# A decoder layer on one core: two per-feature row scales spread by a store and a broadcast read instead of by float32 matmuls with diagonals

## The reference, cut to what matters

```python
mod = silu(c) @ w_ada + b_ada                      # 6 rows of 1024
sh1, sc1, g1, sh2, sc2, g2 = split(mod, 6)
h = rms_norm(x, g_pre_mix) * (1 + sc1) + sh1
o_sb, o_mb, o_ds = three attention variants on h @ w_in      # 6 + 5 + 5 heads
g_sb, g_mb, g_ds = split(sigmoid(gate_logits + b_gate), 3)
merged = g_sb * (o_sb @ w_proj_sb) + g_mb * (o_mb @ w_proj_moba) + g_ds * (o_ds @ w_proj_dsa)
x = x + g1 * rms_norm(merged @ w_o, g_post_mix)    # the first row scale: g1 * g_post_mix
h = rms_norm(x, g_pre_ffn) * (1 + sc2) + sh2
gate, up = split(h @ w_up, 2)
x = x + g2 * rms_norm((silu(gate) * up) @ w_down, g_post_ffn)   # the second: g2 * g_post_ffn
```

## Time and profile before

| | |
|---|---|
| median of three runs | 485.15 us (483.96 to 485.51) |
| the profiled execution | 484.05 us, span on the core 482.3 us |
| TensorE busy | 453.0 us, 94% |
| TensorE's weight load busy | 411.3 us, 85% |
| VectorE busy | 299.8 us, 62% |
| ScalarE busy | 242.5 us, 50% |
| GpSimd busy | 60.4 us, 13% |
| DMA | 98.81 MB, mean 205 GB/s |

### The profile page before, as it was taken

One profiled execution on the slowest core, in us unless ns is written; L12 is line 12 of the kernel. 1 busy time (PEld: TensorE's weight loads), 2 busy tenths in 40 slices (PEclk: granted clock), 3 DMA queues, 4 the chain that ended last, 5 costly groups with the idle time before them and its releaser, 6 DMA issues.

```text
span 482.3 us, 8224 instructions
## 1 busy us (share of the span) xinstructions
PE 453.0 (94%) x3253; PEld 411.3 (85%) x3253; DVE 299.8 (62%) x487; ACT 242.5 (50%) x426; POOL 60.4 (13%) x96
## 2 busy tenths in 40 slices
PE   0959999999989998999999999999999999999994
PEld 0639999999878998998888799999999999999993
DVE  2056778878599968873779547672662464266215
ACT  5055554656656655667456237663353254335232
POOL 2000003000023220003769000000000000000000
PEclk9979999999999999999999999999999999999998
DMA  8998886696676566652466900997545735620002
GB/s 299 424 350 263 299 295 215 207 345 233 241 262 205 172 235 230 217 177 71 139 224 244 370 35 0 341 364 256 198 152 174 258 117 183 225 87 0 1 1 87
DMA packets 56370, 98.81 MB, mean 205 GB/s; under 512 B 5036, under 2 KB 41492, under 8 KB 53268
## 3 DMA queue, kind: packets, MB, share of 16 engines
q1 hardware_dynamic: 54036, 81.62, 49.4%
q0 software_dynamic: 2304, 16.78, 10.0%
HBM read 97.35 MB, written 1.05 MB: 204 GB/s over the span
## 4 chain that ended last, share of the span: by engine, by line
PE 86%; DVE 4%; DMA 4%; issue 2%; ACT 2%; SPq 1%; POOL 1%; DVEq 0%; ACTq 0%; PEldq 0%
PE psum L1163 26%; PE psum L1164 24%; PE psum L1165 24%; DMA ada_end<-in_w_ada_dram 4%; PE psum L1437 3%; DVE wlo L864 1%; PE psum L1390 1%; PE psum L1322 1%; PE psum L1259 1%; PE psum L1215 1%; PE psum L1257 1%; PE psum L1293 1%; PE psum L1226 1%; PE psum L1304 1%; POOL buft L540 1%
## 5 line engine op out<-in xcount | busy, mean ns | idle before, releaser
L1163 PE MATMUL psum<-hhi,whi 128*128 128x256 f32 (+1 forms) x680 | 196.8, 289 | 3.5 <-DVE hlo L968 2.7
L1164 PE MATMUL psum<-hlo,whi 128*128 128x256 f32 (+1 forms) x680 | 193.4, 284 | 0.0
L1165 PE MATMUL psum<-hhi,wlo 128*128 128x256 f32 (+1 forms) x680 | 193.2, 284 | 0.0
L1163 PEld LDWEIGHTS psum<-hhi,whi 128*128 128x128 f32 (+1 forms) x680 | 130.5, 192 | 8.4 <-issue 4.2
L1164 PEld LDWEIGHTS psum<-hlo,whi 128*128 128x128 f32 (+1 forms) x680 | 130.7, 192 | 0.3
L1165 PEld LDWEIGHTS psum<-hhi,wlo 128*128 128x128 f32 (+1 forms) x680 | 130.6, 192 | 0.0
L864 DVE TENSOR_TENSOR wlo<-raw,whi 128x1024 fp32r<-128x1024 f32 (+4 forms) x92 | 92.6, 1037 | 22.0 <-ACT whi L608 21.6
L608 ACT ACTIVATE whi<-raw 128x1024 fp32r<-128x1024 f32 (+4 forms) x92 | 74.3, 843 | 18.7 <-DMA raw<-in_w_in_dram 16.6
L1114 DVE TENSOR_TENSOR dlo<-draw,dhi 128x2048 fp32r<-128x2048 f32 x11 | 25.1, 2292 | 57.1 <-ACT dhi L783 57.1
L1109 DVE TENSOR_TENSOR wlo<-raw,whi 128x1024 fp32r<-128x1024 f32 x40 | 47.0, 1218 | 2.8 <-ACT whi L776 2.8
L783 ACT ACTIVATE dhi<-draw 128x2048 fp32r<-128x2048 f32 x11 | 20.9, 1914 | 43.9 <-PE psum L1165 43.9
(11 more groups left out here) (160 smaller groups left out, 593.7 us busy)
## 6 DMA issues: line engine op xcount, KB each, us to landing
raw<-in_w_up_dram SPq DMA_DIRECT2D x22, 1024.0 KB, 7.7
xn<-in_w_ada_dram POOLq DMA_DIRECT2D x16, 1024.0 KB, 5.2
raw<-in_w_in_dram SPq DMA_DIRECT2D x7, 2048.0 KB, 9.2
draw<-in_w_down_dram SPq DMA_DIRECT2D x11, 1024.0 KB, 5.3
raw<-in_w_in_dram SPq DMA_DIRECT2D x4, 1280.0 KB, 7.1
raw<-in_w_in_dram SPq DMA_DIRECT2D x3, 1536.0 KB, 6.9
raw<-in_w_ada_dram SPq DMA_DIRECT2D x2, 2048.0 KB, 9.8
ada_end<-in_w_ada_dram SPq DMA_DIRECT2D x4, 1024.0 KB, 17.0
```

What stands on the lines that cost most here:

```text
L1163: pe.matmul(dst, a[0], b[0], start=first, stop=False)
L1164: pe.matmul(dst, a[0], b[1], start=False, stop=False)
L1165: return pe.matmul(dst, a[1], b[0], start=False, stop=last)
```

## The change

Both row scales are written to a small tensor in device memory and read back with a broadcast over all partitions. GpSimd issues these DMAs: the store of the first scale in the unit loop at u = 27, behind the work of that unit; the store of the second after the loop; then both reads, once all heads are out, each behind a wait for its store. A store takes eight values from each partition, and their places in device memory are 128 floats apart, so all 1024 values stand alone; a read brings 4 KB to each of 128 partitions. The four diagonals, the four float32 matmuls, the four copies to `gb` and the waits between them are gone. VectorE waits for the arrival of the read before it first uses a scale.

```diff
--- before.py
+++ after.py
@@ -203,8 +203,6 @@
 MERGE_PIECES += [[(f // 2 + 2, 0), (f // 2 + 2, 1)] if f % 2 else [(f // 2 + 1, 2), (f // 2 + 1, 3)] for f in range(1, KC - 1)]
 MERGE_PIECES += [[(KC // 2 + 1, q) for q in range(4)]]
 
-SPREADS = [(1, 0, 0), (1, 0, 1), (2, 1, 0), (2, 1, 1)]
-
 VEC_GATE, VEC_ADA, VEC_PRE_MIX, VEC_POST_MIX, VEC_PRE_FFN, VEC_POST_FFN, VEC_END = (
     0, 3 * KC, 9 * KC, 10 * KC, 11 * KC, 12 * KC, 13 * KC)
 
@@ -283,7 +281,6 @@
         olo = sb("olo", [P, FULL_OCH, S], F32R, scope=mix)
         acc = sb("acc", [P, ADA_COLS], scope=mix)
 
-        spread = [acc[:, BANK * i:BANK * (i + 1)] for i in range(len(SPREADS))]
         mrow = sb("mrow", [P, BANK], scope=mix)
         wix = sb("wix", [P, TT, H_IX], scope=mix)
         dist = sb("dist", [P, CAUSAL], scope=mix)
@@ -344,7 +341,8 @@
         ss_ready, var_ready, sqrt_ready, xn_ready = sem("ss_ready"), sem("var_ready"), sem("sqrt_ready"), sem("xn_ready")
         x_turned, h_act, h_dve, h_hi, h_lo = sem("x_turned"), sem("h_act"), sem("h_dve"), sem("h_hi"), sem("h_lo")
         wix_turned, wix_ready, dve_scaled = sem("wix_turned"), sem("wix_ready"), sem("dve_scaled")
-        col_ready, diag_ready, m_spread, gb_ready = sem("col_ready"), sem("diag_ready"), sem("m_spread"), sem("gb_ready")
+        col_ready = sem("col_ready")
+        gain_out, gain_in = [None, sem("gain_out1"), sem("gain_out2")], [None, sem("gain_in1"), sem("gain_in2")]
         vec_in, vec_turned, vec_ready = sem("vec_in"), sem("vec_turned"), sem("vec_ready")
         logits, relu_ready, score_added, score_masked = (sem("logits"), sem("relu_ready"), sem("score_added"),
                                                         sem("score_masked"))
@@ -396,6 +394,9 @@
                 return [(P, slice(0, 3), every), (P, slice(3, 5), every), (P, slice(5, FULL_OCH), every),
                         (P, slice(FULL_OCH, N_OCH), every)]
             return [(P, slice(q, q + 1), every) for q in range(4)]
+
+        gain_dram = nc.dram_tensor("gains", (3, D), F32).ap()
+        GAIN_COLUMNS = [None, slice(0, KC), slice(KC, 2 * KC)]
 
         def hold(b):
 
@@ -523,6 +524,17 @@
                     pool.wait_ge(acc_done, n)
                 pool.dma_start(ada_part, ada_dram[:, n % KC, ADA_COLS * (1 + n // KC):ADA_COLS * (2 + n // KC)]).then_inc(part_in, 16)
 
+            def store_gain(g):
+
+                pool.wait_ge(col_ready, g + 1)
+                pool.dma_start(gain_dram[g, :].rearrange("(k p) -> p k", p=P), col[g][:, GAIN_COLUMNS[g]],
+                               allow_slow_non_contiguous=True).then_inc(gain_out[g], 16)
+
+            def load_gain(g):
+
+                pool.wait_ge(gain_out[g], 16)
+                pool.dma_start(gb[g][:, :], gain_dram[g:g + 1, :].to_broadcast([P, D])).then_inc(gain_in[g], 16)
+
             load_part(0)
             for u in range(N_UNITS):
                 if u == max(LOGITS_AT):
@@ -552,19 +564,14 @@
                     n = ADA_AT[u]
                     if n + 1 < 2 * KC:
                         load_part(n + 1)
-
-            def spread_diag(i):
-
-                g, vector, half = SPREADS[i]
-                pool.wait_ge(summed, 3)
-                pool.wait_ge(col_ready, g + 1)
-                for c in range(4):
-                    k = KC * vector + 4 * half + c
-                    ins = pool.tensor_scalar(spread[i][:, P * c:P * (c + 1)], ident[:, :], col[g][:, k:k + 1], -1.0, ALU.mult, ALU.mult)
-                ins.then_inc(diag_ready, 1)
-
-            for i in range(3):
-                spread_diag(i)
+                if u == max(min(COLUMNS_AT) + 1, ADA_UNIT[KC] + 1):
+                    store_gain(1)
+
+            store_gain(2)
+
+            pool.wait_ge(o_lo, N_HEADS)
+            load_gain(1)
+            load_gain(2)
 
             def merge_lo(f):
 
@@ -579,9 +586,7 @@
                 pool.wait_ge(gated, 3 * (f + 1))
                 pool.wait_ge(pool_step, f + 1)
                 pool.tensor_tensor(h32[:, f, :], g[0], g[2], ALU.add).then_inc(merged, 1)
-                if f == 0:
-                    spread_diag(3)
-                else:
+                if f:
                     merge_lo(f - 1)
             merge_lo(KC - 1)
 
@@ -759,10 +764,6 @@
                 act.wait_ge(merged, f + 1)
                 act.wait_ge(units, N_UNITS)
                 act.activation(hhi[:, f, :], h32[:, f, :], ACT.Copy).then_inc(m_hi, 1)
-                if 1 <= f <= len(SPREADS):
-                    g, _, half = SPREADS[f - 1]
-                    act.wait_ge(m_spread, f)
-                    act.activation(gb[g][:, BANK * half:BANK * (half + 1)], bank[6 + half][:, :], ACT.Copy).then_inc(gb_ready, 1)
             load_roots()
 
             def cut_up_hi(i, slot, q, first=False):
@@ -1094,7 +1095,7 @@
                     ins.then_inc(dve_scaled, 1)
 
                 if t == 0:
-                    dve.wait_ge(gb_ready, 2 * (k + 1))
+                    dve.wait_ge(gain_in[k + 1], 16)
                 gain(0)
                 if k == 0 and t == 1:
                     modulate(0)
@@ -1204,15 +1205,6 @@
                 for n in range(4):
                     mm = pe.transpose(bank[B_ROWS[g]][:, P * n:P * (n + 1)], mrow[:, P * n:P * (n + 1)], ident[:, :])
                 mm.then_inc(m_turned, 1)
-
-            def spread_gain(i):
-
-                pe.wait_ge(diag_ready, i + 1)
-                if i == 0:
-                    pe.wait_ge(o_lo, N_HEADS)
-                elif i >= 2:
-                    pe.wait_ge(gb_ready, i - 1)
-                pe.matmul(bank[6 + SPREADS[i][2]][:, :], neg1[:, :], spread[i], start=True, stop=True).then_inc(m_spread, 1)
 
             def turn_x(k, t):
 
@@ -1389,9 +1381,6 @@
                             pe.matmul(dst, w[0][:, ch, :], ohi[:, ch, :], start=False, stop=False)
                             mm = pe.matmul(dst, w[1][0:HD, ch, :], ohi[0:HD, ch, :], start=False, stop=True)
                 mm.then_inc(units, 1)
-                if 1 <= f <= len(SPREADS):
-                    spread_gain(f - 1)
-
 
             def out_part(t, half, n, kk):
 
@@ -1400,7 +1389,6 @@
                              [block_view(x[b % 2], b)[:, kk, BANK * n:BANK * (n + 1)] for x in (whi, wlo)],
                              k == 0, k == KC - 1)
 
-            pe.wait_ge(gb_ready, 4)
             for t in range(TT):
                 if t == 1:
                     pe.wait_ge(gated, 3 * KC)
```

## The result

The changed kernel takes 489.62 us (median of four runs, 488.31 to 493.79) against 484.99 for the kernel before (four runs); the ratio is 1.0107, 95% interval 1.0077 to 1.0136. It is slower by about 5 us, where 2.7 us less was forecast. The profiled execution took 489.13 us, span 487.4; that of before 484.05 and 482.3. The two differ by 5.1 us, and all of it is there at the join of TensorE and VectorE after the merge stage: the wait that ended at 267.35 ends at 272.46 (start, us, what, from the chain in order of time).

A forecast was written before the change was run, and what follows sets the result against it. TensorE's chain was taken as the bound, with VectorE and the first w_o load close behind: 3.40 us of matmuls removed, 2.7 us kept, added DMAs zero. 485.15 - 2.7 = 482.45, rounded to 482.4 us; 8-in-10 range 480.4 to 485.0.

The forecast's parts named there:

- What bounds the kernel, and what goes: Merge stage: TensorE's chain loses four gain matmuls, but the first w_o load's landing limits the gain to 2.7 us.
- the full 3.4: Merge stage: four gain matmuls of 0.85 us each, the 3.40 us TensorE alone would bring at the join.
- First store: Ahead of head 6's mask on GpSimd: 5.65 us of cover, so an issue of 4.3 us fits and costs nothing.
- Second store, the wait for its landing: GpSimd at 226.20 us: wait for landing at most 2.1 us after the issue ends; cost zero.
- the issue's cost D: GpSimd's time to issue one scattered store: 0.6 to 4.3 us, taken as about 1 to 2 us.
- my own formula: When the second store and reads free GpSimd: 226.20 + D + 2.1 + 0.54, so 229.4 to 233.1 us.
- the 233.6: Latest start, in us, of GpSimd's sum of tile 0 that still allows the w_o load at 239.5.
- The broadcast data: Two reads, 1.05 MB, beside the projection weights: 2.8 us of transfer, no cost taken, up to 1.4 us as bad end.
- the four that I had named as wrong: Store issue above 5.65 us; longer mask wait near 144; GpSimd in DMA work at 233.6; ScalarE awaiting weights near 234.
- (D): Slower: single-float issue of 8.4 us delays head 6 by 2.75 and the w_o load by 2.2; 490.1 us, chance 0.12.
- (C): Broadcast reads push the third projection block by 1.4 us, leaving 1.3 us saved; 483.85 us, chance 0.17.
- (A): The forecast itself: 2.2 to 3.0 us saved, 482.2 to 483.0 us, chance 0.47.

The follow-up runs named there:

- e1: Changed kernel with the second gain's store and read both moved behind GpSimd's last merge work; 482.10 us.
- e2: Changed kernel with stores as 128 runs of 32 bytes instead of 1024 single floats, all DMAs in place; 483.83 us.
- e4: Kernel before the change plus only the second gain's scattered store at 226 us, no read; 488.54 us.
- e3: Changed kernel with only the second broadcast read moved behind GpSimd's merge work, both stores kept; 489.61 us.
- e5: e1 plus a probe store of 1024 single floats, 512 bytes apart, in the merge stage; 482.62 us.
- e9: e1 plus a probe store of 1024 single floats, 32 bytes apart, in the merge stage; 482.53 us.
- e6: e1 plus a probe store of the scattered pattern cut to 256 floats side by side; 487.70 us.
- e10: e1 plus a probe store of 128 single floats side by side, one from each partition; 487.67 us.
- e7: e1 plus the full scattered store of 1024 floats, issued from ScalarE ahead of its merge work; 489.90 us.
- e8: e1 plus a probe read of 1024 single floats from device memory into SBUF; 482.25 us.

## Why the prediction was wrong, step by step

**What bounds the kernel, and what goes: right.** e1 has the four matmuls, the diagonals and the evictions gone and is free of the store in the merge stage. It is 0.55% faster than before, 2.7 us of 484.98, by the ratio (2.9 by the medians), where 2.7 was forecast. Also the path was the forecast one: the w_o load came at 240.04 with the offset taken off, instead of 240.87 (forecast 239.5), ScalarE waited for its landing, and the join moved by 2.5 us and not by the full 3.4.

**First store: right, and better covered than I knew.** Its issue took 0.94 us, with 5.7 us of room by the rows (143.79 less 138.08; I had written 5.65). It too lands only after 13.1 us, but nobody waits for it before 227: SyncE's issue at 225.47 and the earlier trace rows's 226.20 for the columns (226.23 after) are where they were.

**Second store, the wait for its landing: a term that was mis-sized.** I wrote "the wait for the store's landing, at most 2.1 us after the issue ends by the output stores". It was 11.0 us. The row I took it from is of stores whose rows are 2 KB long. I had looked for both ends of the issue's cost D, where 4.3 us was my bad end and 0.91 the truth. The landing got a single value from a store of another form, without an end above it. With 11.0 in its place my own formula (226.20 + 0.91 + 11.0 + 0.54 = 238.65) gives GpSimd's measured start, 238.71, and 5.1 us past the 233.6 that I had named as the limit. "Both ends of D fit. Cost zero" fell with it.

**The weights beside the store: the step that failed and made the loss.** Under "The broadcast data" I asked what the added DMAs do to the projection weights, looked only at bytes, and wrote "I take no cost", with 1.4 us at worst. The bytes were indeed cheap: e2, with the same reads, lost about that against e1. But the cut that waits for the third projection block came 6 to 8 us later: at 241.61 in the changed kernel and 240.18 in e4, where it was 233.82. e4 has no read, so a transfer of 4 KB did it, not one of 512 KB. That a store could slow loads of other queues was in none of my rivals; I had put it at nothing without asking. e3 shows that it brings the loss without GpSimd's wait (489.61 us). What the wait would cost with the weights in time, no run shows.

**Signs.** Two of the four that I had named as wrong came: GpSimd was still in DMA work at 233.6 (until 238.7), and ScalarE waited for projection weights (in e3, where GpSimd's wait is gone, from 234.8 on). The other two, the store's issue and the mask near 144 us, did not.

**Rivals.** (D) had the sign and a time, 490.1, that lies 0.5 from the measured one, and this is luck. More than half of its 5.0 us was the first store's delay of head 6, which cost nothing, and its cause was an issue of 8.4 us (twice 4.3 is 8.6), which took 0.9. What it had right is the path: GpSimd late, behind it the cuts of the third block and the w_o load (2.2 us late; measured 6.4). (C) had late weights with half of the gain left, at 1.4 us of delay instead of 8. Neither had the clock: in the 7 us without matmuls TensorE's granted clock fell to 0.50, and tile 4, most of which ran at it, took 1.5 us more. (A)'s saving was that of e1.

**The rule of the Trainium skill.** Of the Trainium skill I weighed the rule of one descriptor per element against the statement that generation is a small part. For the issue the second was right: 0.91 to 0.94 us for 1024 floats against 0.54 for 128 rows. The Trainium skill ("DMA: Bandwidth & Descriptors", Specifications) also says that below 512 bytes the engines read, modify and write. e5 and e9 speak against a price on that alone, as 1024 such writes were harmless in both. The same page (Anatomy of one DMA) gives some 2.0 us of fixed cost, mostly the receipt of the write; here the measurement decides, at 9.5 to 13.7 us for the dense stores.

**What stays open.** The mechanism. That the writes go one after the other within 512 bytes is argued from e5, e6, e9 and e10; no trace shows it. e9 doesn't favour it: 16 floats in each 512 bytes landed in 5.3 us, no later than e5's 5.6, where I had expected 1.3 us for them. The stretch that counts could as well be one of 32 bytes: e2 and e9 are harmless, and in both no 32 bytes are written from more than one partition, while in the dense stores eight partitions write into them. Not tried: floats 8 or 16 bytes apart, and whether it takes several DMA engines or one alone would do it. The harm isn't in order of size either: the cut started at 238.64 with 256 floats and at 240.31 with 128, in one trace each. Why loads of another queue are held up meanwhile is open too; the runs show that they are.

## What to carry to other kernels

A DMA has three costs: its issue, its landing, and what it does to the transfers beside it; bound each from rows of the same form (piece length, direction, layout of the target), and where there is no such row, give it a wide upper end, and ask who would wait at that end. Writing a column that lies across 128 partitions as neighbouring floats in device memory is a small transfer that holds up large ones: keep it out of stretches in which weights are just in time, or leave gaps between the floats (with gaps only probes ran here, whose data nobody read back). What is needed late should be sent late: moving the second gain behind the merges turned 5 us lost into 2.7 us won, and this version beats both kernels. And when a DMA is taken out of an engine's order, look where the ones behind it move to, as with the first read in e1.

## What the runs showed of the hardware

- 128 floats from 128 partitions, written side by side into 512 bytes, landed in 9.5 us (e10), 256 in 10.9 (e6), 1024 in 10.3 to 13.7 from GpSimd (e3 has both ends) and in 13.5 from ScalarE (e7). 1024 floats written 32 or 512 bytes apart landed in 5.3 and 5.6 us (e9, e5), 128 runs of 32 bytes side by side in 4.7 and 5.6 (e2), and 1024 floats read from neighbouring places in 5.6 (e8).
- While such a dense store was under way, loads of 384 KB that land in 3.2 us took 11.1 us in the changed kernel and up to 11.2 in e7.
- GpSimd's issue of 1024 single floats took 0.87 to 0.95 us, of 256 0.72, of 128 0.55.
- The changed kernel: TensorE had its last matmul at 240.2 us; its granted clock was 0.96 from 240 to 244, 0.50 from 244 to 250, with matmuls again from 247.29, and 1.00 from 252 on. In e6's trace it was still 0.50 from 250 to 252.
